# Expert rows spread by a bfloat16 one-hot in three exact parts, statistics on ScalarE, and a reordered end of a mixture-of-experts layer

## The reference, cut to what matters

```
y = token_mixing(x * (1 + scale1) + shift1, ...)
x = layer_norm(DEEPNORM_ALPHA * x + gate1 * y, ln_g[0], ln_b[0])
y = hier_moe(x * (1 + scale2) + shift2, ...)
x = layer_norm(DEEPNORM_ALPHA * x + gate2 * y, ln_g[1], ln_b[1])

def hier_moe(h):                       # 16 experts, a token goes to 2 of them
    gate = ...                         # (tokens, 16), two weights a token, else 0
    hid = silu(h @ w_e1[e]) * (h @ w_e3[e])          # 1024 -> 512, each expert e
    return sum over e of gate[:, e] * (hid[e] @ w_e2[e])   # 512 -> 1024
```

## Time and profile before

| | us |
|---|---|
| median of 3 runs | 1371.91 (1368.77 to 1372.64) |
| the profiled execution | 1370.16 |
| its span | 1368.3 |
| PE busy in the span | 1309.3 (96%) |
| DVE / ACT busy | 570.7 (42%) / 241.8 (18%) |
| granted TensorE clock, mean | 0.992 of 2.4 GHz |

### The profile page before, as it was taken

How to read it: one execution, slowest core, us unless ns; L and a number is a source line. 1 busy time by engine, 2 the same in 40 slices (tenths; PEclk the granted TensorE clock), 3 DMA queues, 4 the chain that set the end, 5 groups by cost and what they waited for, 6 DMA issues and landing times. The chain is left out here.

```text
span 1368.3 us, 18611 instructions
## 1 busy us (share of the span) xinstructions
PE 1309.3 (96%) x7388; PEld 797.7 (58%) x7388; DVE 570.7 (42%) x1066; ACT 241.8 (18%) x524; POOL 140.0 (10%) x115
## 2 busy tenths in 40 slices
PE   6999999999999999999979999999999999999994
PEld 2675586478645555555528656856874565555552
DVE  1224454466334622322352345546643454322324
ACT  0021221333301201111010213212330121111110
POOL 0003431022200000000000043401230000000000
PEclk9999999999999999999999999999999999999998
DMA  9854554656549799999963626344544659999982
GB/s 381 306 224 184 208 192 157 250 208 262 240 170 383 288 422 423 426 426 424 414 264 127 242 94 223 131 158 168 214 169 155 254 222 423 425 428 422 423 349 93
DMA packets 46173, 375.32 MB, mean 274 GB/s; under 512 B 15130, under 2 KB 19354, under 8 KB 23196
## 3 DMA queue, kind: packets, MB, share of 16 engines
q1 hardware_dynamic: 37680, 371.14, 67.6%
q10 hardware_dynamic: 8428, 3.29, 0.9%
HBM read 370.07 MB, written 4.33 MB: 274 GB/s over the span
## 5 line engine op out<-in xcount | busy, mean ns | idle before, releaser
L1134 PE MATMUL psum<-ring,hT 128*128 128x512 f32 x512 | 230.8, 599 | 4.1 <-ACT hT L1357 2.2
L1134 PEld LDWEIGHTS psum<-ring,hT 128*128 128x128 f32 x512 | 94.2, 191 | 110.4 <-issue 105.0
L1130 PE MATMUL psum<-hT,ring 128*128 128x256 f32 x640 | 143.1, 380 | 0.0
L1130 PEld LDWEIGHTS psum<-hT,ring 128*128 128x128 f32 x640 | 119.9, 190 | 18.3 <-issue 3.1
L1306 PE MATMUL psum<-ring,tbuf 128*64 128x512 f32 x512 | 116.9, 598 | 2.8 <-ACT tbuf L1574 1.4
L1267 PE MATMUL psum<-ring,tbuf 128*64 128x256 f32 x1024 | 116.8, 381 | 0.0
L1267 PE MATMUL psum<-ch,tbuf 128*64 128x256 f32 x1024 | 113.3, 379 | 0.0
L1267 PEld LDWEIGHTS psum<-ring,tbuf 128*64 128x64 f32 x1024 | 72.1, 137 | 53.6 <-issue 21.3
L2082 DVE TENSOR_SCALAR tbuf<-tbuf 128x256 f32<-128x256 f32 x32 | 9.4, 294 | 224.7 <-ACT tbuf L1564 224.7
L1267 PEld LDWEIGHTS psum<-ch,tbuf 128*64 128x64 f32 x1024 | 73.2, 137 | 43.0 <-issue 8.0
L1158 PE MATMUL psum<-ring,tbuf 128*128 128x512 f32 x192 | 82.7, 592 | 0.0
(11 more groups left out here) (310 smaller groups left out, 1486.9 us busy)
## 6 DMA issues: line engine op xcount, KB each, us to landing
ring<-in_stream SPq DMA_DIRECT2D x125, 2048.0 KB, 9.7
ch<-in_stream SPq DMA_DIRECT2D x36, 2048.0 KB, 10.5
bias_ring<-in_b_in SPq DMA_DIRECT2D x26, 256.0 KB, 8.2
ldata<-in_ldata SPq DMA_DIRECT2D x2, 2329.0 KB, 17.6
tbuf<-in_stream SPq DMA_DIRECT2D x2, 2048.0 KB, 14.7
hbuf<-in_ln SPq DMA_DIRECT2D x4, 1024.0 KB, 9.1
hbuf<-in_stream SPq DMA_DIRECT2D x1, 2048.0 KB, 8.2
ring<-in_stream SPq DMA_DIRECT2D x2, 1024.0 KB, 21.3
```

The lines of the kernel that those rows point to most:

```text
L1130: mm = pe.matmul(psum[:, PJ + g, part * G * P:(part + 1) * G * P], w[:, k, (2 * g + part) * P:(2 * g + part + 1) * P], hT[:, k, :], start= ...
L1134: mm = pe.matmul(bank(PJ + g), hT[:, k, g * P:(g + 1) * P], w[:, k, :], start=(k == 0), stop=(k == KT - 1))
```

## The change

- The selection `e_sel` is a bfloat16 one-hot without the weight. PE turns it by products with a bfloat16 identity, and two products of 3 columns bring the gate weight of each slot beside it, as three bfloat16 parts (`gw_parts`, made once per layer in `weights`).
- DVE multiplies the down result by that weight (`weighted_rows`), and `e_out` is divided into three bfloat16 parts: ACT makes the high one, DVE subtracts, ACT makes the middle one, DVE the low one. The spread is 3 parts x 2 halves x 2 groups of bfloat16 products. It always runs one expert later, cut in two. Only the last expert of a pass keeps the float32 spread (`spread_last`).
- In the first expert DVE runs `pick_pair` ahead of `split_tokens`, then `weighted_rows`, then `silu`.
- SP loads the down matrix of expert 15 ahead of the two modulation matrices. The first chunk of layer 1 is loaded in two halves, as that of layer 0 was.
- After the experts ACT makes the sums and squares (two Copy and one Square with an accumulated sum), and DVE adds all four residual halves first, without BN_STATS. `turn_x` of group 1 moves to q = 1.

```diff
@@ SP
-                if l + 1 < DEPTH:
-                    for j, m in enumerate(LAYER_MODS):
-                        sp.wait_ge(slot_used, used_e(l, 0, NE - 2, j))
-                        sp.dma_start(ahead_slot[j], dram["stream"][stream_slot("mod", l + 1, m)]).then_inc(layer_mods_loaded[j], 16)
                 expert_slot(0, NE - 1, 2, used_e(l, 0, NE - 2, 2))
+                if l + 1 < DEPTH:
+                    for j, m in enumerate(LAYER_MODS):
+                        sp.wait_ge(slot_used, used_e(l, 0, NE - 2, j))
+                        sp.dma_start(ahead_slot[j], dram["stream"][stream_slot("mod", l + 1, m)]).then_inc(layer_mods_loaded[j], 16)
@@ PE, before_first_chunk (layer 1) and the spread
+                    elif q == 1:
+                        turn_x(l, 0, 1, 4)
...
-                def spread_group(n, i, g, opens=False, closes=False):
-                    for hf in range(2):
-                        pe.matmul(bank(Y_MOE[g][hf]), e_selT[i][halves_of[hf], g, :], e_out[halves_of[hf], :], start=opens, stop=closes)\
+                def spread_group(i, g, opens=False):
+                    for s in range(3):
+                        for hf in range(2):
+                            mm = pe.matmul(bank(Y_MOE[g][hf]), e_selT[i][halves_of[hf], g, :], e_parts[halves_of[hf], s, :], start=opens and s == 0, stop=False)
+                            if s == 2:
+                                mm.then_inc(spread, 1)
+                def spread_last(g):
+                    for hf in range(2):
+                        pe.matmul(bank(Y_MOE[g][hf]), e_selT_last[halves_of[hf], g, :], e_out[halves_of[hf], :], start=False, stop=True)\
@@ PE, pair
-                        pe.wait_ge(eout_ready, n)
+                        pe.wait_ge(out_read, n)
                         for g in range(G):
-                            mm = pe.transpose(psum[:, OUT, g * P:(g + 1) * P], e_sel[:, g, :], ident)
+                            pe.matmul(psum[:, OUT, g * P:(g + 1) * P], e_sel[:, g, :], ident_b, start=True, stop=True)
+                        for g in range(G):
+                            mm = pe.matmul(psum[:, OUT, G * P:G * P + 3], e_sel[:, g, :], e_weight[:, g, 0:3], start=(g == 0), stop=(g == G - 1))
                         mm.then_inc(sel_turned, 1)
-                        if i == 0 and not first:
+                        if not (first and i == 0):
                             pe.wait_ge(selT_ready, n)
-                            spread_group(n - 1, 1, 0)
+                            pe.wait_ge(eout_ready, n)
+                            spread_group(1 - i, 0, opens=first)
...
-                        if i == 0 and not first:
-                            spread_group(n - 1, 1, 1)
+                        if not (first and i == 0):
+                            spread_group(1 - i, 1, opens=first)
...
-                        if i == 0 or last:
-                            pe.wait_ge(eout_ready, n + 1)
+                        else:
+                            pe.wait_ge(out_read, n + 1)
                             for g in range(G):
-                                spread_group(n, i, g, opens=first and i == 0, closes=last and i == 1)
+                                spread_last(g)
@@ ACT
-                        act.wait_ge(spread, n * 4)
-                        act.activation(e_out, bank(OUT), ACT.Copy).then_inc(eout_ready, 1)
+                            act.wait_ge(out_read, n + 1)
+                            act.activation(e_parts[:, 0, :], e_out, ACT.Copy).then_inc(out_high, 1)
+                            act.wait_ge(out_left, n + 1)
+                            act.activation(e_parts[:, 1, :], e_out, ACT.Copy).then_inc(out_middle, 1)
@@ DVE
+                def weighted_rows(n, p, e, turned, whole=False):
+                    dve.wait_ge(selT_ready, n + 1)
+                    dve.tensor_reduce(slot_weight, turned[:, G * P:G * P + 3], X, ALU.add).then_inc(slot_weight_read, 1)
...
+                    ts(e_out, bank(OUT), slot_weight, None, ALU.mult).then_inc(out_read, 1)
...
+                    tt(e_out, e_out, e_parts[:, 0, :], ALU.subtract).then_inc(out_left, 1)
...
+                    tt(e_parts[:, 2, :], e_out, e_parts[:, 1, :], ALU.subtract).then_inc(eout_ready, 1)
@@ DVE, first expert of a pair (the second: tokens_in, select, tokens_in, weighted_rows, silu)
                             select(n + 1, e + 1)
-                            if first and isinstance(p, int):
-                                for g in range(G):
-                                    split_tokens(g)
-                            silu(n + 1)
                             if not last:
                                 pick_pair(n + 2, e + 2, e_pick_b)
+                            if first and isinstance(p, int):
+                                for g in range(G):
+                                    split_tokens(g)
+                            weighted_rows(n, p, e, turned_slots[0])
+                            silu(n + 1)
@@ ACT, after the experts
+                def statistics(g):
+                    act.wait_ge(x_added, l * 4 + (2 * g + 1))
+                    link(act.activation(bank(4), x[:, g, 0:W], ACT.Copy, accum_out=x_sum[:, g, 0:1]))
+                    link(act.activation(x_mean[:, g, 0:1], x_sum[:, g, 0:1], ACT.Copy, scale=-1.0 / D))
+                    act.wait_ge(x_added, l * 4 + (2 * g + 2))
+                    link(act.activation(bank(4), x[:, g, W:2 * W], ACT.Copy, accum_out=x_sum[:, g, 1:2]))
+                    link(act.activation(x_mean[:, g, 1:2], x_sum[:, g, 1:2], ACT.Identity, scale=-1.0 / D, bias=x_mean[:, g, 0:1]), ln_mean)
+                    link(act.activation(bank(4, 2), x[:, g, :].rearrange("p (b n) -> p b n", b=2), ACT.Square, bias=x_mean[:, g, 1:2], accum_out=x_square[:, g, :]))
+                    link(act.activation(rstd[:, g, :], x_square[:, g, :], ACT.Ln, scale=1.0 / D, bias=eps))
+                    act.activation(rstd[:, g, :], rstd[:, g, :], ACT.Exp, scale=-0.5).then_inc(ln_rstd, 1)
@@ DVE, after the experts
-                finish(1, 0)
-                residual(1, 1, 0)
+                for g in range(G):
+                    for hf in range(2):
+                        residual(1, g, hf)
+                centre(0)
+                scale_and_shift(0)
+                centre(1)
                 if l + 1 < DEPTH:
                     modulate(l + 1, 0, 0, 2)
-                residual(1, 1, 1)
-                normalise(1, 1)
+                scale_and_shift(1)
```

More of the change, by code:

```diff
@@ L334, in build @@
         rstd = small(G, 1)
+        x_sum, x_mean, x_square, eps = small(G, 2), small(G, 2), small(G, 1), small(1)
         lg = small(G, 20)
@@ L468, in build @@
         ln_var = sem("ln_var")
+        x_added, ln_mean = sem("x_added"), sem("ln_mean")
         ln_rstd = sem("ln_rstd")
@@ L717, in _ @@
                 for i, (kind, _, c) in enumerate(RING_ORDER[l]):
-                    if (kind, c, l) == ("in", 0, 0):
-                        first_chunk(i)
+                    if (kind, c) == ("in", 0):
+                        first_chunk(l, i)
                     else:
@@ L1571, in pair @@
                             act.wait_ge(spread, (n - 1) * 4)
-                        act.activation(e_selT[i].rearrange("p g n -> p (g n)"), psum[:, OUT, 0:G * P], ACT.Copy).then_inc(selT_ready, 1)
+                        turned = turned_last if last and i == 1 else turned_slots[i]
+                        act.activation(turned, psum[:, OUT, 0:G * P + 3], ACT.Copy).then_inc(selT_ready, 1)
                         act.wait_ge(hid_turned, n + 1)
@@ L1603, in _ @@
                 further_passes(act, expert_pass(0), expert_pass, no_pass)
-                for g in range(G):
-                    norm_scale(1, g)
-                    if l + 1 < DEPTH:
-                        modulate(l + 1, 0, g, 2 + 2 * g)
-                        if g == 0:
-                            act.wait_ge(layer_mods_filled, 1)
-                            act.activation(sig, bank(1), ACT.Copy).then_inc(layer_mods_copied, 1)
+                act.wait_ge(spread, (l * PASSES + 1) * (NE * 4) + 4)
+                statistics(0)
+                statistics(1)
+                if l + 1 < DEPTH:
+                    modulate(l + 1, 0, 0, 2)
+                    act.wait_ge(layer_mods_filled, 1)
+                    act.activation(sig, bank(1), ACT.Copy).then_inc(layer_mods_copied, 1)
+                    modulate(l + 1, 0, 1, 4)
                 link.close()
@@ L2106, in pair @@
                             tokens_in(n + 2, 1, XG)
+                            if first and isinstance(p, int):
+                                for g in range(G):
+                                    link(ts(x[:, g, :], x[:, g, :], ALPHA, None, ALU.mult))
+                            weighted_rows(n, p, e + 1, turned_slots[1])
                             silu(n + 1)
+                        else:
+                            weighted_rows(n, p, e + 1, turned_last, whole=True)
```

99 lines of the change are left out of this document (71 added, 28 removed).

## The result

The changed kernel takes **1360.59 us**, median of 4 runs (1358.33 to 1361.20), against 1370.72 (4 runs, 1368.77 to 1372.64) for the one before: a ratio of 0.9929, 95% interval 0.9910 to 0.9948. The forecast was 1362.5.

A forecast was written before the change was run, and what follows sets the result against it. The expert loop was taken as held by memory and PE at once, the rest by DVE, ACT and PE chains. Terms summed to 8.5 us: 1361.7 or 1363.4 by reference, taken as 1362.5, range 1355 to 1369.5.

The forecast's parts named there:

- expert loops: Expert stages up to expert 14's down product: gain of 0.5 us in layer 0 and 0.2 in layer 1, 0.7 together.
- last pairs: Expert 14's down product to expert 15's, both layers: 12.8 us instead of 14.98 and 14.12, a gain of 3.5.
- between the layers: Expert end of layer 0 to layer 1's first chunk: group 0's x 0.9 later, 1.71 wait gone, net gain 0.7.
- `e_out` on DVE: Emptying the bank in the last pairs by DVE instead of ACT, 0.69 for 0.60 us: 0.2 lost over both layers.
- end of the kernel, DVE: Last statistics after layer 1's experts: DVE needs 11.1 us instead of 14.9, a gain of 3.8.
- the 1.4 and 0.4 us: Slack at expert 14's down product, layers 0 and 1: PE started that long after its matrix landed, and could gain it.
- the 0.9 taken off for the first pair: First pair of layer 0: a buffer freed 1.3 us later makes the next load land 0.9 later, subtracted from 1.4.
- Rival A's second branch: Expert loop: the stream has room up to 428 GB/s, 2.1 us less a layer, about 1358; rival A altogether 10%.
- The first pair's delay: First pair of experts: DVE's longer list makes expert 1's down product start at 481.5 instead of 480.19, 1.3 us later.
- Groups: Spread groups of six bfloat16 products, in three side-by-side pairs, last 0.8 us each, 3.2 instead of 4.04 a pair of experts.
- B: Spread groups: bfloat16 halves do not run side by side, 1.45 us a group instead of 0.8, about 1386 in all; 7%.
- so nothing waits: End of layer 0: modulation matrices land by 691 at the latest, PE wants them at 692 and 698, no wait.

The follow-up runs named there:

- `b_half_down`: The kernel before the change, with only the first half of every expert down matrix loaded (1024 KB instead of 2048): 1371.84 us.
- `a_mods_first`: The changed kernel with the old load order at the end of layer 0, both modulation matrices ahead of expert 15's down matrix: 1360.95 us.
- `a_no_branch`: The changed kernel without the conditional further passes on every engine, so it cannot serve an expert with more than 64 tokens: 1357.98 us.
- `a_half_down`: The changed kernel with only the first half of every expert down matrix loaded (1024 KB instead of 2048): 1343.02 us.
- both experiments: The changed kernel without the conditional on any engine, 1357.98 us; and with the last expert's multiplication on ACT instead of DVE, 1359.47 us.
- the last experiment: The changed kernel timed again, 1360.85 us (ratio 0.9943), beside it with the last expert's multiplication on ACT, 1358.23 us (ratio 0.9928).

## Why the prediction was right, and where its terms were not

The total came out 1.9 us off, and the signs hold. That it is so close is partly luck: the loops, the last pairs and the stretch between the layers gave 4.7 us more than forecast, and a missed wait, a later start and smaller items took 4.0 of it back. Its 8.5 us, term by term:

| term | predicted | measured |
|---|---|---|
| expert loops | 0.7 | 3.7 |
| last pairs | 3.5 | 3.9 |
| `e_out` on DVE | -0.2 | -0.45 |
| between the layers | 0.7 | 2.0 |
| wait ahead of the last statistics | none | **-2.4** |
| end of the kernel, DVE | 3.8 | 3.7 |
| start of the stage | none | -1.35 |
| store and rounding | none | 0.1 |
| sum | 8.5 | 9.2 |

**Loop: mis-sized.** "It can't end a stage earlier because PE frees buffers earlier, except by what the slices reached at best" fixed the landings, and left only the 1.4 and 0.4 us by which PE came behind the 42nd. `b_half_down` shows the flaw: the old period was PE's, and the stream kept it. Landings at a period of 4.95 are no proof that the queue could not do 4.90. Against the stage's start the 42nd load now lands 1.75 us earlier in layer 1, and the other 0.33 of the 2.08 is PE's slack: there the faster stream was the answer, near the 2.1 given for 428 GB/s. In layer 0 it lands only 0.45 earlier, and 1.2 of the 1.65 is the slack that the forecast counted, 1.4 (0.23 is left). So in layer 0 the forecast went wrong mainly by the 0.9 taken off for the first pair. The mechanism (PE runs into the loads and gives back the rest) is right: with half the down matrices PE shows the 28.0 that I had at 28.5. Rival A's second branch, 1358 for the stream at 428, thus came nearest for this term, and the missed wait and the later start below took its gain away. The first pair's delay was oversized: the down product of expert 1 comes 0.3 us later against that of expert 0, not 1.3. DVE's list ahead of `weighted_rows` took about 0.7 less than I added up, and the chain 3.6 instead of 3.8.

**Groups and last pairs: right.** Groups pace 0.75 (0.8 predicted; B, at 1.45, falls), pair 29.4, waits of about a microsecond, no wait at the last down product, 12.62 and 12.61 us against 12.8.

**`e_out`.** "0.69 for 0.60" was taken from a DVE operation without a pointer scalar. It is 0.75, and starts 0.1 later.

**Between the layers: mis-sized.** Group 0's x is later, by 1.6 us rather than 0.9, of which 0.74 is the stall of DVE at its third addition. Where it is missing, in `a_mods_first` and `a_no_branch`, x comes 8.46 and 8.48 us after DVE's start, the 8.4 of the forecast; "so nothing waits", said of the modulation matrices, left out what stands behind them. Group 1 is turned earlier and its 1.71 wait is gone: the chunk is 14.71 us instead of 16.66. What I had not seen is the clock. Before, the modulation product ahead of the chunk ran at half clock (3.62 us). In the new kernel the first of the two does (3.51, window clock 0.57), where nothing waits for it, and the second takes 1.92 at clock 1.00: 1.7 us less that no step contained. It comes with the long pause: in six other profiles that have it the second product takes 1.92 to 2.51, in `a_mods_first`, with 2.65 us of pause, 3.62 again. The length of the pause alone does not decide it: in `a_half_down` (2.39) both products are slow, 3.41 and 3.58. No run varied the pause by itself.

**The branch: missed.** I cost "DVE instead of ACT" as one operation against another. The operation was the last in DVE's list ahead of a conditional, so at the end of layer 1 what had been hidden behind ACT came into view: 2.4 us, shown by both experiments. In layer 0 the same step cost nothing.

**End: right.** 11.17 us of DVE against 11.1; ACT's root is ready 0.28 us late and not just ahead.

**The stream's speed.** The window shows 429 GB/s with PE beside it. The Trainium skill (HBM Reference, "Specifications (TRN2)") says that a core that streams alone reaches about 425, and that each gets about 358 when both of a pair stream. The trace agrees with the first, 4 above it, here on one core, and nothing in this study shows the second. The prediction's "in every expert slice" holds but for the last slice of the second stage, 349 GB/s, in which the loads run out.

## What to carry to other kernels

Where two resources have the same period, take work away from one in an experiment or in thought before crediting either: the one that only keeps the other's pace still has room, and here it had nearly 2 us in layer 1. Then look at how the stage starts, since a late start there was carried through. When an operation moves to another engine at the end of that engine's list, cost the branch, wait or loop that the engine used to pass while it was idle, and ask whether its code still has to come, and behind which loads. And look at the granted clock behind every pause of PE next to the change, since a pause that moves shifts which product pays for it.

## What was not expected of the hardware

- A conditional can stop an engine for microseconds. At the end of layer 1 DVE stood 3.50 to 3.71 us between its last operation and the next in all seven profiles in which it did the last multiplication (2.4 more than without the conditional); in layer 0 the same conditional held it for nothing (1.29, as without it). PE stood 2.35 to 4.75 us, by how long loads were still arriving (table above).
- After PE's pause of 4.45 us, the 16 products of 512 columns ran at a granted clock of 0.57, near the lower of its two levels (1.2 of 2.4 GHz), and in 3.51 us rather than 1.92. After 5.61 us without work the window clock was 0.56.
- Two stretches far from the change run at one clock or another from execution to execution: the program's first chunk (9.84 and 8.83 us above), and 32 short products in layer 1, whose rows in the changed kernel and in `a_mods_first` follow. The window 1080 to 1110 us has a clock of 0.94 in the first and 1.00 in the second. The kernel before and both kernels of the last experiment show 5.44 there too. Single executions can't be compared closer than these 1.6 us except stretch by stretch.

```profile
1104.57 5.43 PE L1269 MATMUL psum<-tbuf,ch 128*128 128x128 f32 x32 [0.90 <-DVE tbuf L2129]
```
```profile
1106.09 3.81 PE L1269 MATMUL psum<-tbuf,ch 128*128 128x128 f32 x32 [0.90 <-DVE tbuf L2129]
```

- The loads of a lone core ran at 428 to 429 GB/s over four slices in a row; in a window of 30 us there PE was busy for 96%.
